# Attention pairs in another order: samples' values directly behind samples' scores, S4's low part ahead of a weight difference, an output chunk moved

## The reference, cut to what matters

```python
def sb_core(q, k, v, q_pos, k_pos):
    z = jnp.einsum('bqhd,bkhd->bhqk', q, k, preferred_element_type=jnp.float32) * SB_SCALE
    mask = k_pos[None, :] < q_pos[:, None]
    log_keep = jnp.where(mask, jax.nn.log_sigmoid(-z), 0.0)
    after = lax.cumsum(log_keep, axis=3, reverse=True) - log_keep
    w = jnp.where(mask, jnp.exp(jax.nn.log_sigmoid(z) + after), 0.0)
    return jnp.einsum('bhqk,bkhd->bqhd', w.astype(v.dtype), v)
```

## Time and profile before

| | us |
|---|---|
| median of 3 runs | 2418.31 |
| lowest, highest | 2417.92, 2420.05 |
| profiled execution, own time | 2420.03 |
| profiled execution, span | 2418.3 |
| TensorE busy | 2398.3 (99%) |
| VectorE, ScalarE, GpSimd busy | 1651.9, 1099.8, 449.4 |
| attention pairs, each about | 44.6 |

### The profile page before, as it was taken

How to read it: one execution, slowest core, us unless ns; L and a number is a source line. 1 busy time by engine, 2 the same in 40 slices (tenths; PEclk the granted TensorE clock), 3 DMA queues, 4 the chain that set the end, 5 groups by cost and what they waited for, 6 DMA issues and landing times.

```text
span 2418.3 us, 38739 instructions
## 1 busy us (share of the span) xinstructions
PE 2398.3 (99%) x15340; PEld 2158.1 (89%) x15340; DVE 1651.9 (68%) x2168; ACT 1099.8 (45%) x1779; POOL 449.4 (19%) x386
## 2 busy tenths in 40 slices
PE   9999999999999999999999999999999999999998
PEld 8999999999999998999999988777776899999987
DVE  7766666886665676886666662667666886666667
ACT  5433344354433343643344333767665443344343
POOL 3221113122121110221111101122223321121100
PEclk9999999999999999999999999999999999999999
DMA  4322223223323233142233225898997132222231
GB/s 140 114 77 72 88 88 96 62 79 105 88 70 88 88 98 96 36 122 74 84 89 93 80 80 146 207 218 216 223 228 195 36 116 84 88 88 87 79 99 70
DMA packets 427780, 259.16 MB, mean 107 GB/s; under 512 B 77457, under 2 KB 389777, under 8 KB 427600
## 3 DMA queue, kind: packets, MB, share of 16 engines
q1 hardware_dynamic: 422496, 239.64, 35.8%
q0 software_dynamic: 5104, 17.04, 2.2%
HBM read 248.22 MB, written 8.42 MB: 106 GB/s over the span
## 4 chain that ended last, share of the span: by engine, by line
PE 95%; DVE 2%; ACT 1%; issue 1%; DMA 1%; POOL 0%; SPq 0%; DVEq 0%; ACTq 0%
PE ps L2789 84%; PE ps L833 6%; PE ps L865 2%; PE ps L2838 2%; PE ps L943 1%; DMA raw<-in_ffn_w_dram 0%; DVE x L2156 0%; ACT wt L1758 0%; ACT e_buf L1733 0%; PE ps L856 0%; DVE e_buf L2484 0%; DVE small L2097 0%; DMA x<-in_x_prompt_dram 0%; DVE x L2165 0%; DVE ring L2050 0%
## 5 line engine op out<-in xcount | busy, mean ns | idle before, releaser
L2789 PE MATMUL ps<-xt_hi,ring 128*128 128x320 f32 (+2 forms) x3328 | 782.3, 311 | 1.3 <-DVE ring L2065 0.7
L2789 PEld LDWEIGHTS ps<-xt_hi,ring 128*128 128x128 f32 x3328 | 568.8, 188 | 11.6 <-issue 7.6
L2789 PE MATMUL ps<-ring,h_hi 128*128 128x512 f32 x1760 | 552.0, 391 | 0.0
L2050 DVE TENSOR_TENSOR ring<-raw,ring 128x1024 fp32r<-128x1024 f32 (+1 forms) x317 | 432.3, 1370 | 123.9 <-ACT ring L1448 123.4
L2789 PE MATMUL ps<-xt_lo,ring 128*128 128x320 f32 (+2 forms) x1664 | 514.7, 309 | 0.0
L2789 PE MATMUL ps<-s_ops,ring 128*128 128x320 f32 x3168 | 506.4, 310 | 1.4 <-DVE s_ops L2229 1.2
L2789 PEld LDWEIGHTS ps<-s_ops,ring 128*128 128x128 f32 x3168 | 474.8, 188 | 2.5 <-DVE s_ops L2229 1.4
L2789 PEld LDWEIGHTS ps<-ring,h_hi 128*128 128x128 f32 x1760 | 330.5, 188 | 69.1 <-DVE x L2139 0.8
L1448 ACT ACTIVATE ring<-raw 128x1024 fp32r<-128x1024 f32 (+1 forms) x317 | 285.9, 931 | 228.6 <-PE ps L2789 211.9
L1229 POOL TENSOR_TENSOR t_buf<-raw,t_buf 128x512 f32<-128x512 f32 x88 | 115.0, 1307 | 1331.9 <-DVE t_buf L2092 1331.9
L2789 PE MATMUL ps<-ring,h_lo 128*128 128x512 f32 x880 | 343.4, 390 | 0.0
(11 more groups left out here) (211 smaller groups left out, 2478.5 us busy)
## 6 DMA issues: line engine op xcount, KB each, us to landing
raw<-in_ffn_w_dram SPq DMA_DIRECT2D x263, 512.0 KB, 4.1
v_raw<-in_cache_v_dram SPq DMA_DIRECT2D x128, 256.0 KB, 4.1
k_raw<-in_cache_k_dram SPq DMA_DIRECT2D x96, 256.0 KB, 5.6
raw<-in_sb_w_in_dram SPq DMA_DIRECT2D x24, 512.0 KB, 5.0
raw<-in_ple_w_gate_dram SPq DMA_DIRECT2D x16, 512.0 KB, 4.1
k_raw<-in_cache_k_dram SPq DMA_DIRECT2D x128, 64.0 KB, 3.9
g_b<-in_ln_g_dram POOLq DMA_DIRECT2D x8, 512.0 KB, 5.6
b_b<-in_ln_b_dram POOLq DMA_DIRECT2D x8, 512.0 KB, 7.5
```

Of the source, the lines that this page charges most:

```text
L2050: ve.tensor_tensor(ring[:, slot, 1, col:col + cols], conversion_source(u), ring[:, slot, 0, col:col + cols].bitcast(F32), ALU.subtract).th ...
L2789: return pe.matmul(out, w, xx, start=first, stop=last, skip_group_check=True)
```

## The change

It moves calls; nothing is added or taken away. In pairs 0 to 6: the previous pair's values of unit 8 and the own totals come directly behind `scores(i, 2)`, ahead of `suffix(i, 0)` and of the two key planes (pair 0 has no such values, only the totals); at the end of the pair the values of unit 5 come directly behind `scores(i, 9)`, ahead of the next pair's first two key planes. The last pair keeps its order. VectorE's copies of `tot` and of key plane 1 change places with that. In the SwiGLU stage that follows the pooling, S4b's lo part comes ahead of the second difference on VectorE. Behind the last pair, chunk 6 of tile 0 of the output product comes behind suffix 9 and values 8.

```diff
 STEP_EVENTS = {
-    2: [("kT", 1, 0), ("kT", 1, 1), ("tot",)],
+    2: [("tot",), ("kT", 1, 0), ("kT", 1, 1)],
...
+LAST_TOTALS = [("kT", 1, 0), ("kT", 1, 1), ("tot",)]
...
-    for event in STEP_EVENTS.get(u, []):
+    for event in LAST_TOTALS if (i, u) == (PAIRS - 1, 2) else STEP_EVENTS.get(u, []):
...
                 scores(i, 2)
                 if follows:
+                    if i:
+                        values(i - 1, 8)
+                    own_totals(i, ("tot",))
                     suffix(i, 0)
-                turn_keys(i, 1, 0)
-                if not follows:
+                    turn_keys(i, 1, 0)
+                else:
+                    turn_keys(i, 1, 0)
                     suffix(i, 0, (0,))
-                if i:
                     values(i - 1, 8)
-                if not follows:
                     suffix(i, 0, (1,))
-                own_totals(i, ("tot",))
+                    own_totals(i, ("tot",))
...
                 suffix(i, 7)
                 scores(i, 9)
+                values(i, 5)
                 if follows:
                     turn_keys(i + 1, 0, 0)
-                values(i, 5)
                 if follows:
                     keys_to_tokens(i + 1, ("kt4",))
                     keys_to_tokens(i + 1, ("kt1",))
...
             values(last, 7)
-            out_early(0, range(4, DC - 1))
+            out_early(0, range(4, 6))
             suffix(last, 9)
             values(last, 8)
+            out_early(0, range(6, DC - 1))
             out_early(1)
...
-                    first_diffs(st, 1)
-                    low_right43(prev, "S4b")
+                    if prev.kind == "pool":
+                        low_right43(prev, "S4b")
+                        first_diffs(st, 1)
+                    else:
+                        first_diffs(st, 1)
+                        low_right43(prev, "S4b")
...
-                    turned(i, 1, 0)
-                    evacuate_event((i, ("tot",)))
+                    if follows:
+                        evacuate_event((i, ("tot",)))
+                        turned(i, 1, 0)
+                    else:
+                        turned(i, 1, 0)
+                        evacuate_event((i, ("tot",)))
```

## The result

| | us |
|---|---|
| before, median of 19 runs | 2418.76 (2417.48 to 2421.25) |
| changed, median of 19 runs | 2422.55 (2421.64 to 2424.80) |
| ratio changed to before | 1.0014, 95% interval 1.0008 to 1.0021 |
| changed, profiled execution, own time and span | 2423.27 and 2421.5 |

The account below looks back on a forecast made before the run. It took TensorE, busy 2398.3 of 2418.3 us, to bound the kernel. Terms +2.1, +0.45, +2.4, +0.3 and -0.55 summed to +4.7 us, on the median 2418.31 giving 2423.0 us, range 2418.0 to 2426.0.

Parts of the forecast that it names:

- place 1: Samples' scores to unit 3's scores, pairs 1 to 6: TensorE waits for ScalarE, +0.35 us a pair, +2.1 in all.
- The last step: Start of the key transposes to unit 3's scores, pairs 1 to 6: 1.78 us, set by ScalarE's copy and weights.
- the scores: Samples' scores to the values behind them, pairs 1 to 6: 0.85 us.
- the totals: Own totals to suffix, pairs 1 to 6: between 0.24 and 0.40 us, 0.24 at the low end.
- third rival: Own totals and the step ahead keep their traced cost: 0.66 us lost a pair, +6.7 in all, 2425.0 us; chance 0.17.
- the high values 1.07 and 0.40: Upper ends in us, pairs 1 to 6: values to own totals 1.07, own totals to suffix 0.40.
- Pair 0: First pair, samples' scores to unit 3's scores: second key plane waits for VectorE's 0.14 us totals copy, +0.45 us.
- Place 2: End of pairs 0 to 6: own keys' transposes wait for the key copies, +0.34 us each, +2.4 in all.
- S4b: Stage behind the pooling, low part ahead of the difference: +0.3 us, with -1.0 and +0.4 as ends.
- fourth rival: Behind the pooling, the load after the moved difference lands early: +3.4 us in all, 2421.7 us; chance 0.15.
- The chunk: Output chunk 6 of tile 0 behind the last pair: -0.55 us, with -0.4 and -0.8 as ends.
- first rival: Attention, S4b and chunk: drains decide and ScalarE's copies are not awaited, -6.8 us, 2411.5 us; chance 0.09.

Follow-up runs that it names:

- e4_weights_first: Changed kernel with ScalarE's weights of unit 0 ahead of its first key plane copy in pairs 1 to 6; 2418.30 against 2419.58 us for the kernel before.
- e1_place1: Kernel before with only values of unit 8 and own totals moved directly behind samples' scores, pairs 0 to 6; 2421.33 against 2419.58 us.
- e2_place2: Kernel before with only values of unit 5 moved ahead of the next pair's two key planes; 2421.79 against 2419.58 us.
- e8_swap_alone: Kernel before with only ScalarE's weights of unit 0 put ahead of its first key plane copy, pairs 1 to 6; 2422.00 against 2419.47 us.
- e6_best: Kernel before with totals move and ScalarE swap (pairs 1 to 6), own keys' transposes later at pair ends, S4b's low and chunk 6 moved; 2418.23 against 2419.47 us.

## Why the prediction was right, and where not

- **ScalarE decides at place 1: right.** The last step is 1.78 us as taken over from pair 0, and e4_weights_first shows by taking that order away that this was the cause. Forecast +0.35 a pair, measured +0.31. The steps were off by 0.03 each way: the scores take 0.88 (I had 0.85 from the last pair), the totals 0.21 (0.24). The third rival, with the high values 1.07 and 0.40, is refuted: both were waits for ScalarE, as the prediction suspected.
- **Pair 0: right**, +0.45 forecast and measured. The totals' copy took the 0.14 us given to it.
- **Place 2: right**, +0.34 forecast and measured; the transposes waited 0.34 us for ScalarE's key copy, and the fifth for VectorE's.
- **S4b: wrong.** The failed step is "If the chain moves as one, 517.13 becomes 517.53". It did not: the load went out 0.29 us later (507.62) and the difference came 0.74 sooner, since VectorE's order decided, as the fourth rival had it. The term was +0.3 and measured -0.65 between the profiles, about -0.35 against undisturbed executions of the old order. There is no wait at 517 either, where the prediction expected 1.5 us. I had read one execution's chain, with an instruction transfer in it, as the rule. Nor was the won 1.3 us kept: 0.7 went into the wait at 509, for which the prediction has no term. The trace of the kernel before shows GpSimd's sums from 504.60 to 507.25 and VectorE's product with two SBUF inputs at 507.83; won time moves the product in among the sums.
- **The chunk: right**, -0.55 forecast, -0.6 measured.
- **The sum**: +4.4 us without S4b against some +4.1 measured; with it +4.7 against +3.2 to +3.8. The fourth rival, +3.4 with a chance of 0.15, is nearer in number and in mechanism. That the total still came out near my forecast is because the term that failed is a small one: it is wrong by 0.65 to 0.95 us of 4.7. The measured 0.14% lies within the 0.2% that had 0.53.
- **The first rival**, that only the drains count, named a real gain: its 3.67 us is nearly the 3.69 that e4_weights_first measures. What it lacked was ScalarE's order, which the change didn't touch.

## What to carry over

Before work is moved on the busy engine, look at the order of the idle one that frees its banks: here its copy and its weights had to change places with the move, and either half alone lost 0.3 us a pair while both together won 0.5. Work that stands between a producer and a bank's next user is a cover; if it is moved, price the copy that it covered. And where a term rests on a wait that one execution shows, ask whether a transfer that comes and goes (instructions) is part of it.

## What the runs showed of the hardware

- A change of tile shape behind samples' scores costs 0.12 us (1.00 against 0.88), not the 0.15 that I had worked out.
- Between 440 and 475 us, far from every edit up to there, TensorE lost a little over 1 us in some executions and not in others. Windows of TensorE (columns: stretch, its length, busy us and instructions, granted clock, DMA share, GB/s), first of before, then of e1_place1:

```profile
465.00:470.00 5.00, 5.00 (x33) 0.74 0.02 3
470.00:475.00 5.00, 5.00 (x40) 0.92 0.00 0
```

```profile
465.00:470.00 5.00, 5.00 (x41) 1.00 0.01 3
470.00:475.00 5.00, 5.00 (x45) 1.00 0.00 0
```

  A mean of 0.74 over 5 us is the granted clock at its lower level (1.2 of 2.4 GHz) for about half of that stretch. TensorE had been busy without a break in the slices ahead of it. In the changed kernel the fall stands at 460 to 465 (0.66). Eight of the twelve profiles have it. Those of e1_place1, e2_place2 and e8_swap_alone don't and gain 1.0 to 1.45 us on before in this stretch, which is why their spans alone would flatter them. That of e6_best doesn't have it either, but TensorE stood 0.72 us for ScalarE at 461 there, and nothing is gained. What starts it wasn't tried and stays open.
- GpSimd and VectorE: the block of a whole instruction by the other engine's, told above, 1.52 against 0.49 us. The profile shows it as a long instruction of the blocked engine and not as idle time, so no view of waits names it.
